# Expert products as three fp16 products of halves, with the expert weights halved during the input projection

## The reference, cut to what matters

```python
proj = rmsnorm(x) @ w_in                      # 1024 x 3080
x = x + mixer(proj) @ w_out                   # RG-LRU and gated-delta heads
h = rmsnorm(x)
# top group of 4, then top 2 of its 8 experts; the rows of an expert are padded to blocks of 128
y = (silu(xblk @ w1[e]) * (xblk @ w3[e])) @ w2[e]     # w1, w3: 1024 x 256, w2: 256 x 1024
out = rmsnorm(x + weighted sum of a token's two y)
```

## Time and profile before

| | |
|---|---|
| median of 3 runs | 3889.58 us (3886.83 to 3892.31) |
| span of the profiled execution | 3880.7 us (the profile gives no other time of this execution) |
| TensorE busy | 3414.8 us, 88% of the span |
| VectorE, ScalarE, GpSimd busy | 1815.5, 1315.1, 822.7 us |
| moved by DMA | 513.88 MB, 132 GB/s over the span |

### The profile page before, as it was taken

The page is one execution under the profiler, slowest core; times in us unless marked ns, Lnnn a source line. Parts: engine busy times, 40 slices in busy tenths (PEclk is TensorE's granted clock), DMA queues, the critical chain, the costliest instruction groups (busy, mean ns, idle before and its releaser), DMA issues. The chain is left out here.

```text
span 3880.7 us, 57463 instructions
## 1 busy us (share of the span) xinstructions
PE 3414.8 (88%) x17482; PEld 2028.4 (52%) x17483; DVE 1815.5 (47%) x4755; ACT 1315.1 (34%) x2585; POOL 822.7 (21%) x1002
## 2 busy tenths in 40 slices
PE   7999999999996789999999999679999999999920
PEld 3444444444445677777777766434444444444410
DVE  6564464465364547777677767411111111111148
ACT  7465365355355233333333343111111111111122
POOL 0000000000000235555444554111111111111145
PEclk9999999999997589999999999889999999999965
DMA  4311111111112254455554443145555456553268
GB/s 144 120 38 49 65 41 51 59 46 51 38 49 74 92 147 137 141 146 140 144 145 138 131 125 115 55 176 200 205 205 200 176 224 233 194 198 126 87 256 334
DMA packets 335720, 513.88 MB, mean 132 GB/s; under 512 B 79968, under 2 KB 228928, under 8 KB 327104
## 3 DMA queue, kind: packets, MB, share of 16 engines
q1 hardware_dynamic: 252400, 279.19, 23.0%
q10 hardware_dynamic: 54288, 146.56, 9.6%
q0 software_dynamic: 28864, 86.09, 6.4%
HBM read 341.49 MB, written 170.26 MB: 132 GB/s over the span
## 5 line engine op out<-in xcount | busy, mean ns | idle before, releaser
L1778 PE MATMUL ebank<-w,rowsT 128*128 x1568 | 705.0, 603 | 34.0 <-SPq L1719 30.7
L300 PE MATMUL pP<-h_hi,w_hi 128*128 128x512 f16 (+1 forms) x1728 | 625.4, 365 | 31.2 <-DVE h_lo L482 16.9
L300 PE MATMUL pP<-h_lo,w_hi 128*128 128x512 f16 (+1 forms) x1728 | 625.2, 365 | 0.0
L300 PE MATMUL pP<-h_hi,w_lo 128*128 128x512 f16 (+1 forms) x1728 | 624.9, 365 | 0.0
L1778 PEld LDWEIGHTS ebank<-w,rowsT 128*128 128x128 f32 x1568 | 301.8, 193 | 423.0 <-issue 423.0
L1845 DVE TENSOR_TENSOR gu<-ebank,sil 128x256 f32<-128x256 f32 x98 | 41.6, 425 | 698.9 <-ACT sil L1813 698.9
L1796 PE MATMUL ebank<-w,guT 128*128 x784 | 353.4, 594 | 2.6 <-ACT guT L1817 2.6
L513 DVE SCALAR_TENSOR_TENSOR cv<-win,cols_sb,cv 128x512 f32<-128x512 f32 (+1 forms) x432 | 305.4, 707 | 35.1 <-issue 3.6
L1813 ACT ACTIVATE sil<-ebank 128x256 f32<-128x256 f32 x98 | 37.6, 383 | 821.3 <-PE ebank L1778 821.3
L300 PEld LDWEIGHTS pP<-h_hi,w_hi 128*128 128x128 f16 x1728 | 172.4, 100 | 219.3 <-issue 28.9
L300 PEld LDWEIGHTS pP<-h_lo,w_hi 128*128 128x128 f16 x1728 | 172.6, 100 | 186.2 <-issue 11.2
(11 more groups left out here) (336 smaller groups left out, 6149.0 us busy)
## 6 DMA issues: line engine op xcount, KB each, us to landing
w<-in_w SPq DMA_DIRECT2D x32, 2048.0 KB, 9.0
y<-yb ACTq DMA_DIRECT2D x98, 512.0 KB, 4.9
ft<-mixin SPq DMA_DIRECT2D x33, 1280.0 KB, 8.2
mixin<-qo ACTq DMA_DIRECT2D x128, 256.0 KB, 2.0
w<-in_w SPq DMA_DIRECT2D x32, 1024.0 KB, 12.2
xt<-in_x SPq DMA_DIRECT2D x33, 512.0 KB, 5.3
xr<-in_x SPq DMA_DIRECT2D x33, 512.0 KB, 5.3
x<-x2b ACTq DMA_DIRECT2D x33, 512.0 KB, 5.7
```

The lines of the kernel that those rows point to most:

```text
L300: ins = nc.tensor.matmul(pP[n % NPB][:, 0:N], w[:, k, c0:c0 + P], h[:, k, 0:N], start=(k + i == 0), stop=(k == KD - 1 and i == 2))
L1778: ins = nc.tensor.matmul((M0, M1)[p][:, :], xT[p][:, k, :], w13[:, bass.ds(s, 1), k * 512:(k + 1) * 512].rearrange("p a n -> p (a n)"), st ...
```

## The change

The expert weights are halved on the chip. Each expert's 6144 columns are cut in 12 pieces of 512. SyncE loads a raw piece (256 KB) into one of four stage slots, ScalarE writes the fp16 hi half and VectorE the lo half into one of two `halves` buffers, and SyncE stores the buffer (256 KB) to DRAM, where `split` holds all 384 pieces. This is done in projection groups 1 to 7, four pieces (P) at each of 14 places of `sequence()`, 56 in a group and 48 in the last. experts_phase loads the halves from `split` (the same number of bytes, in rows of 2 KB), makes fp16 halves of the gathered rows and of the gated product too, and runs three fp16 matmuls for each fp32 one. The order in `EXPERTS` is turned: gT, T, up, then d0 and d1. The constant matrices are loaded at the start of mix_phase; the projection has only the identity.

```diff
+PW = 512
+PIECES = (W13 + W2) // PW
+PER_GROUP = 56
+NRAW, NHALF = 4, 2
 def sequence():
+    free = iter(range(PER_GROUP))
+    four = lambda: [("P", next(free)) for _ in range(4)]
...
-           ("Q", 2), ("S", 1), ("O", 3)]
+           ("Q", 2), ("S", 1), ("O", 3)] + four()
     for m in range(3, QC):
-        out += [("Q", m), ("S", m - 1)] + [("N", 0)] * (m == 6) + [("B", 0)] * (m == 9)
-    return out + [("Z", 0), ("S", QC - 1), ("Z", 1), ("Z", 2), ("Z", 3)]
+        out += [("Q", m), ("S", m - 1)] + [("N", 0)] * (m == 6) + [("B", 0)] * (m == 9) + four()
+    return (out + [("Z", 0), ("S", QC - 1)] + four() + [("Z", 1)] + four() + [("Z", 2)] + four() + [("Z", 3)] + four())
...
-        stage = sb("stage", [P, 2, KD, P])
+        stage = sb("stage", [P, NRAW, PW])
+        halves = [sb(f"halves{n}", [P, 2, PW], FP16) for n in range(NHALF)]
...
-            sp.dma_start(const[:, :, :], T["mats"]).then_inc(setup_in, 16)
+            sp.dma_start(ident_sb[:, :], T["mats"][:, MATS.index("ident"), :]).then_inc(setup_in, 16)
...
+            def raw(n, i):
+                sp.dma_start(stage[:, i % NRAW, :], T["raw"][bass.ds(n, 1)].rearrange("a p n -> p (a n)")
+                             ).then_inc(raw_in[i % NRAW], 16)
+            def pieces(base, count, following):
+                for i in range(count):
+                    sp.wait_ge(lo_done, base + i + 1)
+                    sp.dma_start(T["split"][bass.ds(base + i, 1)].rearrange("a p b n -> p (a b) n"), halves[i % NHALF][:, :, :]
+                                 ).then_inc(halves_out[i % NHALF], 16)
+                    if i < following:
+                        raw(base + i + NRAW, i)
+            sp.wait_ge(w_split, len(wblocks))
+            for i in range(NRAW):
+                raw(i, i)
             with sp.Fori(2, groups) as g:
                 load(g, GT)
+                pieces((g - 2) * PER_GROUP, PER_GROUP, PER_GROUP)
             load(groups, 1)
+            rest = NE * PIECES - (groups - 2) * PER_GROUP
+            pieces((groups - 2) * PER_GROUP, rest, rest - NRAW)
...
+            def piece_hi(g, i):
+                act.wait_ge(raw_in[i % NRAW], (g - 1) * (PER_GROUP // NRAW * 16) + (i // NRAW + 1) * 16)
+                act.wait_ge(halves_out[i % NHALF], (g - 1) * (PER_GROUP // NHALF * 16) + (i // NHALF + 1) * 16)
+                nc.scalar.activation(halves[i % NHALF][:, 0, :], stage[:, i % NRAW, :], ACT.Copy, scale=W_SCALE
+                                     ).then_inc(hi_done, 1)
...
+            def piece_lo(g, i):
+                dve.wait_ge(hi_done, (g - 1) * PER_GROUP + i + 1)
+                nc.vector.scalar_tensor_tensor(halves[i % NHALF][:, 1, :], stage[:, i % NRAW, :], W_SCALE,
+                                               halves[i % NHALF][:, 0, :], ALU.mult, ALU.subtract).then_inc(lo_done, 1)
...
             with act.Fori(1, groups - 1) as g:
-                group(g, GT, False, GT)
-            group(groups - 1, GT, False, 1)
+                group(g, GT, False, GT, pieces=PER_GROUP)
+            group(groups - 1, GT, False, 1, pieces=NE * PIECES - (groups - 2) * PER_GROUP)
...
+            early_load(0)
+            sp.dma_start(const[:, :, :], T["mats"]).then_inc(const_in, 16)
-            for f in range(len(pre)):
+            for f in range(1, len(pre)):
                 early_load(f)
...
+            pe.wait_ge(const_in, 16)
+            pool.wait_ge(const_in, 16)
+            dve.wait_ge(const_in, 16)
...
 EXPERTS = """
-M.up.pe M.silu.act M.mul.dve
-O.gT.pe O.gTc.act
-T.T0.pe T.T1.pe T.T0c.act T.T1c.dve
+O.gT.pe O.gh.act O.gl.dve
+T.T0.pe T.T1.pe T.T0h.act T.T0l.dve T.T1h.act T.T1l.dve
+M.up.pe M.silu.act M.mul.dve
 O.d0.pe O.d1.pe O.d0c.act O.d1c.dve O.st.act
...
 def load_expert(engine, T, weights, e, p):
-    w13, w2, loaded = weights
-    for dst, src in ((w13, "w13"), (w2, "w2")):
-        engine.dma_start(dst[:, p, :], T[src][bass.ds(e, 1)].rearrange("a p n -> p (a n)")).then_inc(loaded[p], 16)
+    w, loaded = weights
+    for half in range(2):
+        c = half * (PIECES // 2)
+        src = T["split"][bass.ds(e * PIECES + c, PIECES // 2)].rearrange("a p b n -> p a b n")
+        engine.dma_start(w[:, p, c:c + PIECES // 2, :, :], src).then_inc(loaded[p], 16)
...
                     for k in range(KD):
-                        ins = nc.tensor.matmul((M0, M1)[p][:, :], xT[p][:, k, :],
-                                               w13[:, bass.ds(s, 1), k * 512:(k + 1) * 512].rearrange("p a n -> p (a n)"),
-                                               start=(k == 0), stop=(k == KD - 1))
+                        for i, (x, half) in enumerate(((xh, 0), (xl, 0), (xh, 1))):
+                            ins = nc.tensor.matmul((M0, M1)[p][:, :], x[p][:, k, :],
+                                                   w[:, bass.ds(s, 1), k, half, :].rearrange("p a n -> p (a n)"),
+                                                   start=(k + i == 0), stop=(k == KD - 1 and i == 2))
...
                     for k in range(FE // P):
-                        w = w2[:, bass.ds(pe_slot[0], 1), k * D + h * 512:k * D + h * 512 + 512]
-                        ins = nc.tensor.matmul((OA, OB)[h][:, :], guT[p][:, k, :], w.rearrange("p a n -> p (a n)"),
-                                               start=(k == 0), stop=(k == FE // P - 1))
+                        for i, (g, half) in enumerate(((gh, 0), (gl, 0), (gh, 1))):
+                            down = w[:, bass.ds(pe_slot[0], 1), W13 // PW + 2 * k + h, half, :]
+                            ins = nc.tensor.matmul((OA, OB)[h][:, :], g[p][:, k, :], down.rearrange("p a n -> p (a n)"),
+                                                   start=(k + i == 0), stop=(k == FE // P - 1 and i == 2))
```

More of the change, by code:

```diff
@@ L127, in project_phase @@
         w_lo = sb("w_lo", [P, KD, IN], FP16)
-        stage = sb("stage", [P, 2, KD, P])
+        stage = sb("stage", [P, NRAW, PW])
+        w_stage = [stage[:, 2 * n:2 * n + 2, :].rearrange("p a n -> p (a n)").rearrange("p (k n) -> p k n", k=KD)
+                   for n in range(2)]
+        halves = [sb(f"halves{n}", [P, 2, PW], FP16) for n in range(NHALF)]
         xt = sb("xt", [P, GT, D])
@@ L200, in project_phase @@
         carries_ready = sem("carries_ready")
+        raw_in = [sem(f"raw_in{n}") for n in range(NRAW)]
+        hi_done = sem("piece_hi")
+        lo_done = sem("piece_lo")
+        halves_out = [sem(f"halves_out{n}") for n in range(NHALF)]
         table_out = sem("table_out")
@@ L355, in split, with group @@
                 act.wait_ge(weights_in[n % 2], 16 * (n // 2 + 1))
-                nc.scalar.activation(w_hi[:, :, c:c + w], stage[:, n % 2, :, 0:w], ACT.Copy, scale=W_SCALE
+                nc.scalar.activation(w_hi[:, :, c:c + w], w_stage[n % 2][:, :, 0:w], ACT.Copy, scale=W_SCALE
                                      ).then_inc(w_hi_ready, 1)
-            def group(g, nt, stream, following, first=False):
+            def piece_hi(g, i):
[3 more added lines that the diff above has]
+                                     ).then_inc(hi_done, 1)
+            def group(g, nt, stream, following, first=False, pieces=0):
                 N = nt * P
@@ L373, in group @@
                         norm(g + 1, following)
+                    elif kind == "P" and m < pieces:
+                        piece_hi(g, m)
                     elif kind == "Y":
@@ L428, in group @@
                         nc.scalar.activation(alog1[:, 0:nt], aexp[:, 0:nt], ACT.Ln, bias=1.0).then_inc(*act_did.did("B0"))
-            for s in qo_out:
+            for s in qo_out + halves_out:
                 act.sem_inc(s, 16)
@@ L489, in group @@
                         norm(g + 1, following)
+                    elif kind == "P" and m < pieces:
+                        piece_lo(g, m)
                     elif kind in "XQ":
@@ L1664, in sem @@
             return ctx.enter_context(nc.semaphore(name))
-        w13, w2, loaded = weights
+        w, loaded = weights
         idx = [sb(f"idx{p}", [P, 1], I32) for p in range(2)]
         xb = [sb(f"rows{p}", [P, D]) for p in range(2)]
-        xT = [sb(f"rowsT{p}", [P, KD, P]) for p in range(2)]
+        xh = [sb(f"rowsT_hi{p}", [P, KD, P], FP16) for p in range(2)]
+        xl = [sb(f"rowsT_lo{p}", [P, KD, P], FP16) for p in range(2)]
         sil = [sb(f"sil{p}", [P, FE]) for p in range(2)]
         gu = [sb(f"gu{p}", [P, FE]) for p in range(2)]
-        guT = [sb(f"guT{p}", [P, FE // P, P]) for p in range(2)]
+        gh = [sb(f"guT_hi{p}", [P, FE // P, P], FP16) for p in range(2)]
+        gl = [sb(f"guT_lo{p}", [P, FE // P, P], FP16) for p in range(2)]
         yb = [sb(f"yb{p}", [P, D]) for p in range(2)]
@@ L2086 @@
         "ln2_row": a["ln2_g"].reshape(1, D), "final_row": a["final_g"].reshape(1, D),
-        "w13": w13.reshape(NE, P, W13), "w2": w2.reshape(NE, P, W2),
+        "raw": np.concatenate([w13.reshape(NE, P, W13), w2.reshape(NE, P, W2)], 2).reshape(NE, P, PIECES, PW
```

(4 more changed lines are left out.)

71 lines of the change are left out of this document (43 added, 28 removed).

## The result

The changed kernel takes 4240.9 us (median of 4 runs, 4224.96 to 4244.58) against 3890.94 us for the kernel before: a ratio of 1.0894, with an interval of 1.0873 to 1.0915. It is slower, as forecast, inside the range, but by 350 us where I had forecast 181. My own forecast, 4000 to 4170, missed it; the range up to 4260 took it in because it had been widened for the rivals of the long landing and of the clock. The profiled execution has a span of 4242.9 us, 362 more than before; my sum for it was 4062.

What follows compares the result with a forecast made beforehand. TensorE was taken to bound projection and experts, except where weights are late. 3880.7 + 401 (halving) - 222 (experts) + 2 (constants) = 4062 us, 4071 with the 8.9 us to the median; range 4000 to 4260.

Steps and rivals of the forecast that it cites:

- the long landing: Rival, projection: a store of halves waits behind a raw load, landing 3.5 us, a group loses 79 us, 4220 us; chance 0.12.
- the clock: Rival, projection's piece stretch: TensorE's idles lower its clock, about 27 us more a group, 4260 us; chance 0.06.
- The mechanism: Projection groups 1 to 7: waits for stores on two buffers delay a group by 57.2 us, 401 us together.
- the rival of hidden pieces: Rival, projection: stores never hold ScalarE, a group loses perhaps 3 us, 3690 us, faster; chance 0.10.
- then 0.86 us because SyncE issues two DMAs a piece: Projection, each four pieces: the fourth conversion follows the third by 0.86 us, the time of two DMA issues.
- L: Projection: landing of a store of halves, from the end of VectorE's subtraction to ScalarE's start, taken as 2.2 us.
- Reads of the raw pieces are issued four ahead and bind nowhere: Projection: loads of raw pieces hold nothing up; no cost was put on them.
- the low clock: Projection, start of each next group: TensorE begins with a low clock after idling, 1.8 us, seven times.
- The saving by matmuls: Expert blocks: 36 fp16 matmuls replace 24 fp32 records, 8.86 us a block, 2.55 less; 98 blocks save 250 us.
- Late weights: Experts: shorter blocks cover loads less; 14 two-block experts idle 3.4 us, 28 us more in all; three blocks still cover.
- The constants: Mixing phase's start: loading the constants there puts one more transfer ahead of its first steps, 2 us (0 to 5).
- The cover of the new order: Expert blocks: the new order hides a conversion and a subtraction under matmuls, up to 1.3 us a block without it.

Runs made afterwards that it cites:

- the spread run: Changed kernel with four half buffers and a group's 56 pieces put in other places, one to four behind steps from the group's start on: 3832.0 us, ratio 0.985.

## Why the prediction was right, and where its size was off

**The mechanism** was the forecast one: the conversion of the third piece waits for the first store, in ScalarE's own order, ahead of the evacuation. The row L396 shows it. With four buffers ScalarE waits for raw pieces in its place, and without raw loads some of it comes back (140.5 us). The busy shares had spoken for the rival of hidden pieces; by the earlier trace rows the work would have fitted, and after the change ScalarE and VectorE still are at 104 and 112 us of 225.

**The term that was mis-sized** is the step "then 0.86 us because SyncE issues two DMAs a piece ... and the fourth piece needs the second store". It took 2.21 us. L for the first store was right (2.21 against 2.2). Over the 60 fours ahead of Z0 in groups 1 to 6 the second store goes out 1.11 us after the first (median) and lands in 2.99 us, the first in 2.04; without raw loads these are 0.60, 2.09 and 2.03. So the sentence that failed with it is "Reads of the raw pieces are issued four ahead and bind nowhere": ScalarE's conversions wait for none of them, as forecast, but for stores that they make late, and that I had put at nothing. In the middle group of the table of stretches (82.2 us longer than before, where 59.0 were forecast) the difference adds up, by ScalarE's times: seven q chunks at +1.29 (9.0), the first four and those of Q6, Q9 and Z0 at +1.2 to +1.9 (5.9), the three steps behind Z0 at 26.5 us in place of 21.2 (5.3), where the first store of a four lands late too (2.8 us at the median), 3.9 us of idle ahead of the next `h_hi`, less 1.0 at the group's start, where the low clock (0.72 granted over the first 10 us) cost some 0.8 us and not 1.8: 23.1 of the 23.2.

**The rival of the longer landing** (0.12, 4220 us) had the better number and half of the cause: it named the 200 MB and a store that waits behind a raw load. Its place was wrong: SyncE's queue holds a part of it only, and in the q stretch it is not the first landing that is longer, but the second. The Trainium skill (DMA: Bandwidth & Descriptors, "Anatomy of one DMA — SWDGE (gpsimd) path") gives, by its fit for GpSimd's DMAs, an estimate of 2.6 us for each store. The median here is 2.7 beside raw loads and 2.0 without them, so its fit agrees only where the traffic happens to lengthen the landing.

**The clock.** The granted clock is 0.85 in the group and 0.71 to 0.83 in the q stretch, means between its levels of 2.4 and 1.2 GHz, against 1.00; TensorE idles some 3 us between chunks there. The Trainium skill (TensorE: Matmul & The Clock Gate, "A second HAM failure mode: psum-queue depth-cycling") says that small idles between groups of matmuls that cycle through PSUM banks make the clock swing. The trace agrees. But in a q stretch TensorE still idles 3 us of 10, so the chain and not the clock sets the time, and that rival's 4260 us came near by luck.

**The experts.** The saving by matmuls was exact (8.86 us a block). Late weights cost more than I took: between the issues at 3160.90 and 3865.96 lie the same 27 intervals with 69 blocks, 705.1 us for 69 x 8.86 = 611.3, so 94 us are lost in place of 44, +50 where I had +28. The 14 experts of two blocks have 39 of it: their idle is 3.5 to 4.5 us, once 7.2, and not 3.4. The 11 of three blocks, which I had said would still cover the load, have 10: ahead of the next expert's up stand idles of 0.35 to 1.16 us, with the sequencer's loads in front and no releaser named. That is 22 of the 36 us missing from the saving. The other 14 lie in the 29 blocks outside these intervals, which saved 61 us in place of 29 x 2.55 = 74; I did not find out why. They are not in the halving, since without it the rest of the change is worth 191 us and not 220.

**The constants** cost what I had put. From the mixing phase's first load (SyncE's issue) to TensorE's first product with a constant are 7.31 us, against 5.37 before: 1.94 for the 2.

**The cover of the new order** was named in the prediction, with up to 1.3 us a block if it were gone. The run without it lost 1.38 in the block shown, and 114 / 98 = 1.2 us on average. That the numbers meet is luck: the idle for a conversion and a subtraction, which I had named, is 0.28 us, and the larger idle, up to 0.75, stands behind the sequencer's loads, which I had not seen.

## What to carry to other kernels

Cheap background work is bought by its buffers and its traffic, not by the busy shares of the engines that do it: here 70 us of conversions and subtractions a group cost 82 us of delay, of which two more buffers and a spread over the group took back three quarters. Where work waits on a DMA inside the order of an engine that also feeds TensorE, cost every landing beside the traffic that the change itself adds: here the second store took 2.99 us and not 2.2. And a change of precision that brings its own hand-overs should be timed with and without the reordering that hides them: the order was worth 25 us alone and some 114 us with the three products.

## What the runs showed of the hardware that was not expected

At each return of the group loop ScalarE idled with no tile to wait for. The first step of group 4 in the changed kernel, and the instruction queue's packets, MB and share between 843 and 846 us:

```profile
844.88 1.26 ACT L403 ACTIVATE h_hi<-pT,ln 128x512 f16<-128x512 f32 x2 [3.87 <-issue]
```

```profile
q14 instruction: 5, 0.04, 5.1%
```

The same idle is 2.99 to 3.87 us five times here, 2.1 to 2.3 and 2.7 us in the two runs without raw loads, and 4.0 to 5.5 us in the spread run, whose DMA engines are busier (a mean share of 0.66 in a group, against 0.50). It is gone where the code runs on without a branch (group 7, which is written behind the loop, at 1515.53 us), and it did not show before, where that step waits 1 us for TensorE. The instruction queue moved 168 packets, against 87 before and without the halving. The Trainium skill (Runtime: NRT & Kernel Launch, "Instruction fetch mechanics") says that a taken branch to code outside the resident window stalls until it is fetched by DMA; the rows agree, but no run here changed the length of the loop alone.

A second: 256 KB stores whose median landing is 2.0 us without raw loads took 2.7 where the DMA share of the piece stretches is 0.8 to 0.9, and 3.8 where it reaches 1.03. A third: from the first of the two table loads (0.30 us each) to up's first matmul TensorE's sequencer took 1.93 us at the median; ahead of up TensorE idled without a named releaser 81 times in the old order of steps, and 15 times in the new.

What was left open is why a spread group still takes 166 us and not 143: the DMA engines' mean share is 0.66 there, and more raw buffers were not tried.
